# Two transformer blocks on one core: where the gates of the first block's modulation are summed, and in which order a mixer rounds its weights

## The reference, cut to what matters

```python
cond = jax.nn.silu(c)
mod = cond @ ada_w[l] + ada_b[l]
sh1, sc1, g1, sh2, sc2, g2, sh3, sc3, g3 = jnp.split(mod, N_MOD, axis=-1)
hn = _modulate(_rms_norm(h, norm_g[l, 0]), sh1, sc1)
h = h + 0.5 * g1[:, None, :] * _swiglu(hn, ffn1_w_in[l], ffn1_w_out[l])
hn = _modulate(_rms_norm(h, norm_g[l, 1]), sh2, sc2)
z = hn @ w_in[l]
```

## Time and profile before

| | |
|---|---|
| median of 3 runs | 2385.27 us (2381.89 to 2386.27) |
| the profiled execution | 2385.51 us, of which the span 2383.8 us |
| busy in the span | TensorE 2280.7, VectorE 1602.8, ScalarE 1124.5, GpSimd 121.3 us |
| mean granted clock of TensorE | 0.979 |
| read from HBM | 450.43 MB, 189 GB/s over the span |
| modulation tiles loaded | 128 of 512 KB |

### The profile page before, as it was taken

One profiled execution on the slowest core, in us unless ns is written; L12 is line 12 of the kernel. 1 busy time (PEld: TensorE's weight loads), 2 busy tenths in 40 slices (PEclk: granted clock), 3 DMA queues, 4 the chain that ended last, 5 costly groups with the idle time before them and its releaser, 6 DMA issues.

```text
span 2383.8 us, 31741 instructions
## 1 busy us (share of the span) xinstructions
PE 2280.7 (96%) x11796; PEld 1909.4 (80%) x11796; DVE 1602.8 (67%) x1813; ACT 1124.5 (47%) x1307; POOL 121.3 (5%) x174
## 2 busy tenths in 40 slices
PE   5999899999999999999999999999999999999998
PEld 3787787787788787688878889988888888998887
DVE  5886884777677687565565668686566556868655
ACT  2444454434444455444344366654445446665443
POOL 1000033000000004200000000000000000000000
PEclk9999998999999988999999999999999999999999
DMA  8896652687588473356555554446555555434553
GB/s 291 298 315 207 202 179 95 212 284 248 167 297 282 152 242 129 97 194 193 177 194 180 190 159 128 139 150 204 189 180 194 187 184 142 141 124 159 194 192 108
DMA packets 321381, 452.76 MB, mean 190 GB/s; under 512 B 32423, under 2 KB 269833, under 8 KB 320265
## 3 DMA queue, kind: packets, MB, share of 16 engines
q1 hardware_dynamic: 318232, 440.96, 56.3%
q0 software_dynamic: 2784, 9.50, 1.2%
q10 hardware_dynamic: 274, 1.06, 0.1%
HBM read 450.43 MB, written 1.05 MB: 189 GB/s over the span
## 4 chain that ended last, share of the span: by engine, by line
PE 85%; DVE 8%; ACT 3%; issue 2%; POOL 2%; POOLq 0%; DMA 0%; DVEq 0%; ACTq 0%
PE ps L558 19%; PE ps L560 19%; PE ps L559 19%; PE ps L551 4%; PE ps L552 4%; PE ps L553 4%; DVE wlo L1750 2%; PE ps L1038 2%; PE ps L662 1%; POOL side L2443 1%; PE ps L644 1%; PE ps L790 1%; PE ps L645 1%; PE ps L647 1%; PE ps L591 1%
## 5 line engine op out<-in xcount | busy, mean ns | idle before, releaser
L1750 DVE TENSOR_TENSOR wlo<-raw,whi 128x2048 fp32r<-128x2048 f32 (+1 forms) x348 | 791.6, 2278 | 396.2 <-ACT whi L1170 392.7
L1170 ACT ACTIVATE whi<-raw 128x2048 fp32r<-128x2048 f32 x346 | 660.0, 1910 | 282.3 <-PE ps L560 238.9
L558 PE MATMUL ps<-whi,xl 128*128 128x512 f32 x1472 | 593.6, 403 | 3.6 <-DVE u L1929 3.6
L560 PE MATMUL ps<-whi,xh 128*128 128x512 f32 x1472 | 575.2, 391 | 0.0
L559 PE MATMUL ps<-wlo,xh 128*128 128x512 f32 x1472 | 574.9, 391 | 0.0
L558 PEld LDWEIGHTS ps<-whi,xl 128*128 128x128 f32 x1472 | 277.2, 188 | 65.7 <-issue 4.8
L560 PEld LDWEIGHTS ps<-whi,xh 128*128 128x128 f32 x1472 | 277.1, 188 | 60.1
L559 PEld LDWEIGHTS ps<-wlo,xh 128*128 128x128 f32 x1472 | 277.5, 189 | 59.0 <-issue 4.8
L551 PE MATMUL ps<-xl,whi 128*128 128x256 f32 x864 | 254.4, 294 | 17.1 <-DVE wlo L1750 17.1
L558 PE MATMUL ps<-whi,hidl 128*128 128x512 f32 x640 | 252.2, 394 | 0.0
L560 PE MATMUL ps<-whi,hidh 128*128 128x512 f32 x640 | 249.2, 389 | 0.0
(11 more groups left out here) (375 smaller groups left out, 2553.6 us busy)
## 6 DMA issues: line engine op xcount, KB each, us to landing
raw<-in_ffn_w_in_dram SPq DMA_DIRECT2D x176, 512.0 KB
arena<-in_ada_w_dram SPq DMA_DIRECT2D x128, 512.0 KB, 5.7
raw<-in_w_in_dram SPq DMA_DIRECT2D x54, 1024.0 KB
raw<-in_ffn_w_out_dram SPq DMA_DIRECT2D x44, 1024.0 KB
raw<-in_w_ffn_gate_dram SPq DMA_DIRECT2D x88, 512.0 KB
raw<-in_w_ffn_up_dram SPq DMA_DIRECT2D x88, 512.0 KB
raw<-in_w_ffn_down_dram SPq DMA_DIRECT2D x44, 1024.0 KB
raw<-in_w_out_dram SPq DMA_DIRECT2D x16, 1024.0 KB
```

Of the source, the lines that this page charges most:

```text
L558: pe.matmul(o, al, wh, start=start, stop=False, **kw)
L560: return pe.matmul(o, ah, wh, start=False, stop=stop, **kw)
L1170: act.activation(whi[:, k % 3, :], raw[:, k % 3, :], ACT.Copy).then_inc(hi_done, 1)
L1750: tt(a[0], a[1], a[2].bitcast(F32), ALU.subtract).then_inc(lo_done, 1)
```

## The change

Sub-layers 2 and 5 take the gate path that n = 0 has (`GATED`), so the mixers 1 and 4 sum 16 tiles instead of 24 and make four pieces instead of six. `ADAM` counts the tiles of all sub-layers before m, `SUMS` the pieces. In a mixer SP puts two tile loads behind each of units 3, 4, 6, 8, 9, 10, 11 and 12, VectorE does tile sum 4 (and 5) later, rounds unit 5 inside the layer norm, with the forget logits right behind it, and its other roundings stand at other places; ScalarE rounds unit 6 ahead of the wait for the logits and unit 7 behind the square. In n = 5 the loops of VectorE and SP take the form with two groups to a turn. GpSimd zeroes and loads `accg` again in n = 2 and 5.

The counts:

```diff
+GATED = (0, 2, 5)
+ADAM = (0, 0, 24, 40, 64, 88, 104)
...
-        SUMS = (0, 4) + tuple(4 + 6 * i for i in range(1, 6))
+        SUMS = (0, 4, 10, 14, 20, 26, 30)
```

SP in the feed-forwards:

```diff
-                            if n == 0 and two is not None:
-                                sp.wait_ge(adag_used, 2 * two + (odd + 1))
+                            if n in GATED and two is not None:
+                                sp.wait_ge(adag_used, 2 * two + (KC * GATED.index(n) + odd + 1))
...
-                        if m:
+                        if m or n in GATED:
                             group(0)
                             with sp.Fori(0, KC // 2) as two:
```

SP in the mixers:

```diff
-                        for q in (2 * i - 6, 2 * i - 5):
-                            if 0 <= q < 24:
-                                sp.wait_ge(adam_used, 24 * (m - 1) + q + 1)
...
+                        first = {3: 0, 4: 2, 6: 4, 8: 6, 9: 8, 10: 10, 11: 12, 12: 14}
+                        for q in range(first[i], first[i] + 2) if i in first else ():
+                            sp.wait_ge(adam_used, ADAM[m] + q + 1)
...
+                            at = 3072 * (m % 3) + 1024 * (q % 2)
```

TensorE in the feed-forwards (`gate0` stands in the last group):

```diff
-            def gate0(q):
+            def gate0(n, q):
+                e = GATED.index(n)
                 if q == 0:
-                    pe.wait_ge(adag_used, KC + 1)
-                    pe.wait_ge(mod_read, SUMS[1] + 6)
+                    pe.wait_ge(adag_used, KC * (e + 1) + 1)
+                    if n < 5:
+                        pe.wait_ge(mod_read, SUMS[n + 2])
...
-                if n == 0:
-                    pe.wait_ge(gate0_read, 2)
+                if n in GATED:
+                    pe.wait_ge(gate0_read, 2 * GATED.index(n) + 2)
```

TensorE in the mixers:

```diff
                 project(2, 1).then_inc(unit_used, 1)
-                modulation(m, 4)
                 pe.wait_ge(s["o"], seq(L, OUTS, 4))
                 project(3, 0)
-                modulation(m, 5)
                 project(3, 1).then_inc(unit_used, 1)
```

ScalarE in the feed-forwards:

```diff
-                if n == 0:
-                    gate0(0)
-                    gate0(1)
+                if n in GATED:
+                    gate0(n, 0)
+                    gate0(n, 1)
```

ScalarE in the mixers (left out are three functions of the forget logits, then the square of dq and dk):

```diff
                 hi(L, k0 + 5)
                 copy(3)
+                hi(L, k0 + 6)
                 act.wait_ge(s["fx"], l + 1)
...
-                hi(L, k0 + 6)
                 copy(4)
-                hi(L, k0 + 7)
                 copy(5)
...
+                hi(L, k0 + 7)
                 rs(st, L.event(0), sq8h[1], stat2)
...
                 hi(L, k0 + 15)
-                summed(m, 4)
-                summed(m, 5)
```

VectorE in the feed-forwards:

```diff
-                    if n == 0 and two is not None:
-                        ada_gate(2 * two + odd)
-                if m:
+                    if n in GATED and two is not None:
+                        ada_gate(GATED.index(n), 2 * two + odd)
+                if m or n in GATED:
```

VectorE in the mixers (left out in turn: the product and the statistics; the root and the rest of the norm; the cumulated logits; the addition after the spatial mixing; the load of ypad):

```diff
                 gelu_in(1, zt["gv"], zt["cg"])
-                tiles(4, 5)
                 dve.wait_ge(s["gu_e"], 2 * l + 1)
...
+                lo(L, k0 + 5)
+                copied(L, zi["f"])
+                f, w = zt["f"][0:4, 0:S], zt["f"][0:4, S:2 * S]
+                ts(f, f, fb[0:4, l:l + 1], None, ALU.add).then_inc(s["fx"], 1)
...
-                tiles(5, 6)
-                lo(L, k0 + 5)
...
-                tiles(6, 8)
+                lo(L, k0 + 6)
+                tiles(4, 6)
+                lo(L, k0 + 7)
                 dve.wait_ge(s["fl"], l + 1)
...
-                lo(L, k0 + 6)
-                tiles(8, 10)
-                lo(L, k0 + 7)
...
-                tiles(10, 12)
                 head_norm(0, sq8h[1], diffg, ("dq", "dk"), "diffqk")
                 lo(L, k0 + 8)
-                tiles(12, 14)
-                lo(L, k0 + 9)
+                tiles(6, 8)
...
+                lo(L, k0 + 9)
                 logits(L, st, 0, S0, amask, 32 ** -0.5)
-                tiles(14, 16)
+                tiles(8, 10)
...
                 logits(L, st, 1, S1, amask, 32 ** -0.5)
-                tiles(16, 18)
+                tiles(10, 12)
...
                 gelu_in(2, zt["gu"], zt["dq"])
-                tiles(18, 20)
+                tiles(12, 13)
...
                 logits(L, st, 2, S1, amask, 1.0)
-                tiles(20, 21)
+                tiles(13, 14)
...
-                tiles(21, 22)
+                tiles(14, 15)
...
                 rest_out(L, 2, 0, 2, s0f[:, 1024:1536])
-                tiles(22, 24)
+                tiles(15, 16)
                 lo(L, k0 + 13)
```

GpSimd, after `next_gain`:

```diff
                 next_gain(n)
+                if n and n in GATED:
+                    st(pool.memset(accg, 0.0))
+                    at = 3072 * (n % 3) + 2048
+                    pool.dma_start(accg[0:1, :], ada_b[n // 3:n // 3 + 1, at:at + 1024]).then_inc(accg_init, 16)
```

More of the change, by code:

```diff
@@ L415, in tile_of @@
                             q = 3 * odd + t
-                            sp.wait_ge(adam_used, 24 * (m - 1) + 6 * two + (q + 1))
+                            sp.wait_ge(adam_used, ADAM[m] + 6 * two + (q + 1))
                             sp.sem_inc(sp_waited, 1)
@@ L754, in ffn @@
                 group(0, k, GROUPS - 3, (lambda q: modulation(m, q)) if m else None)
-                group(0, k + 3, GROUPS - 2, (lambda q: gate0(q) if q < 2 else None) if n == 0 else None, True)
+                group(0, k + 3, GROUPS - 2, (lambda q: gate0(n, q) if q < 2 else None) if n in GATED else None, True)
                 k += 7
@@ L1299, in summed, with gate0 @@
                                    scale=1.0 if m % 3 == 1 else 0.5).then_inc(mod_read, 1)
-            def gate0(q):
-                act.wait_ge(gate0_summed, q + 1)
-                act.activation(gate[:, 0, 512 * q:512 * q + 512], ps[:, MB, :], ACT.Copy,
+            def gate0(n, q):
+                act.wait_ge(gate0_summed, 2 * GATED.index(n) + q + 1)
+                act.activation(gate[:, n % 2, 512 * q:512 * q + 512], ps[:, MB, :], ACT.Copy,
                                scale=0.5).then_inc(gate0_read, 1)
@@ L1895, in ada, with ada_gate @@
             def ada(m, q, two=0):
-                at, k = q % 2, 2 * two + q // 3
-                dve.wait_ge(adam_loaded[at], (16 * (12 * (m - 1) + q // 2 + 1)) + 48 * two)
+                parts = 2 if m in (2, 5) else 3
+                at, k = q % 2, 2 * two + q // parts
+                dve.wait_ge(adam_loaded[at], (16 * (ADAM[m] // 2 + q // 2 + 1)) + 48 * two)
                 if q == 0:
                     dve.wait_ge(acc_init, 16 * m)
-                dve.wait_ge(adam_used, 24 * (m - 1) + 6 * two + (q + 2))
-                seg = acc[:, 1024 * (q % 3):1024 * (q % 3) + 1024]
+                dve.wait_ge(adam_used, ADAM[m] + 6 * two + (q + 2))
+                seg = acc[:, 1024 * (q % parts):1024 * (q % parts) + 1024]
                 scalar = condT[:, 2, bass.ds(k, 1)]
                 stt(seg, adam[:, at, :], scalar, seg, ALU.mult, ALU.add).then_inc(adam_used, 1)
-            def ada_gate(k):
-                dve.wait_ge(adag_loaded, 16 * k + 16)
-                dve.wait_ge(accg_init, 16)
-                dve.wait_ge(adag_used, k + 1)
+            def ada_gate(e, k):
+                dve.wait_ge(adag_loaded, 16 * k + (16 * KC * e + 16))
+                dve.wait_ge(accg_init, 16 * e + 16)
+                dve.wait_ge(adag_used, k + (KC * e + 1))
                 stt(accg, adag, condT[:, 2, bass.ds(k, 1)], accg, ALU.mult, ALU.add).then_inc(adag_used, 1)
```

23 lines of the change are left out of this document (10 added, 13 removed).

## The result

| | before | after |
|---|---|---|
| median | 2385.77 us of 4 runs (2381.89 to 2387.99) | 2367.35 us of 4 runs (2362.95 to 2371.32) |
| profiled execution | 2385.51 us, span 2383.8 | 2371.32 us, span 2369.6 |
| mean granted clock | 0.979 | 0.982 |

The ratio is 0.9930, its 95% interval 0.9911 to 0.9949: faster by 0.7%. The forecast was 2369.5 us, in a range of 2363 to 2378.

A forecast was written before the change was run, and what follows sets the result against it. TensorE, busy 2280.7 of 2383.8 us, was taken as the bound, its largest hole in the first mixer at unit 5. Per mixer 7.2 + 1.0 + 1.4 - 1.7 = 7.9 us, twice 15.8: 2385.3 to 2369.5 us, range 2363 to 2378.

The forecast's parts named there:

- Rounding inside the norm: Mixers 1 and 4: unit 5 rounded before TensorE needs it, so head sums start 7.2 us sooner; bounds 4.7 and 7.8.
- Does it last: After the head sums: `diffqk` done at 300.8, ahead of its scores at 301.6, a thin cover.
- The rival of a half coming back: `diffqk` or unit 10's late weights open the next hole, 3 to 4 us a mixer; 2376.5 us, chance 0.14.
- SP's loads: Unit 10's load goes out 3.3 us later, its user comes 7 us earlier; ScalarE waits 1 to 2 us before the softmax.
- An idle ScalarE for `raw`: One of the listed signs that would show the prediction wrong; no size given.
- TensorE's cost at nothing: Unit 10's late load costs TensorE nothing, with 3.5 us of slack; at most 3.3 us a mixer without that cover.
- One tile less among the taps: Last stretch of taps: three tile sums instead of four beside GpSimd's diagonals gain 1.0 us a mixer.
- The mixer's end: Last two gate sums leave the mixer, so the next sub-layer's root comes 1.4 us sooner; bounds 0.9 and 1.7.
- The feed-forwards' pieces: Gate sums moved into n = 2 and n = 5 cost TensorE 2 x 0.86 us, 1.7 us lost in each.
- The sum: Each mixer with its feed-forward gains 7.9 us; two make 15.8 us, giving 2369.5 us.
- one rival: The clock falls elsewhere: a shifted mixer gains or loses 2 to 3 us; 2375.5 or 2363.5 us, chance against 0.07.

The follow-up runs named there:

- x2: Kernel before with only the new order of roundings and logits in mixers 1 and 4, all 24 tiles and loads as before: 2417.26 us, ratio 1.0144.
- x1: Changed kernel with the old order of roundings put back in mixers 1 and 4, the gates staying moved: 2376.09 us, ratio 0.9979 to the kernel before.
- x12: Changed kernel with ScalarE's old order alone (unit 6 behind the logits' functions, unit 7 ahead of the square): 2368.74 us, ratio 0.9933 to the kernel before.
- x5: Kernel before with the new order, SP's tile loads and VectorE's tile sums moved too, 24 tiles a mixer kept: 2380.90 us, ratio 0.9981.
- x3: Changed kernel with SP's tiles 8 and 9 behind unit 10's load and later pairs moved later: 2365.26 us, ratio 0.9924 to the kernel before.
- x10: Changed kernel with taps 8 to 13 earlier, last two tile sums later, and SP's tiles 8 to 15 behind the loads of units 10 to 13: 2354.41 us.
- x11: As x5, but with SP's tiles 8 to 13 behind unit 10's load: 2383.01 us, ratio 0.9991 to the kernel before.
- x7: Changed kernel with each gate tile of n = 2 and 5 summed twice on VectorE: 2365.03 us, ratio 0.9921 to the kernel before.
- x8: Changed kernel with each mixer's last two tile sums behind GpSimd's last diagonal: 2359.52 us, ratio 0.9895 to the kernel before.
- x9: Changed kernel with taps 8 to 13 ahead of the second head sums and the last two tile sums behind GpSimd's last diagonal: 2356.51 us.

## Why the prediction was right, point by point

**Rounding inside the norm: right at the head sums, too much at the mixer's end.** Head sums predicted at 288.2, measured at 288.12; 7.2 us forecast, 7.2 and 7.5 measured. The steps too: rounding of unit 5 ends at 279.3 (279.5), the norm at 283.9 (284.2). x2 shows that the order alone does it, x1 that the tiles' places bring 1.7 to 2.4 us without it, x12 that ScalarE's part is some 1 us of it. But the forecast carried the 7.2 us to the mixer's end as the order's share of 9.6. x1 says that the order is worth 3.5 us (ledger) to 5.8 us (ratios) on top of lighter mixers, and x5 that with all 24 tiles it is worth 4.0. Each half of the change needs the other, and the sum came right because the forecast was for both together.

**Does it last: right, on the stated cover.** `diffqk` was forecast for 300.8 and ended at about 300.4, the scores started at 301.53, forecast 301.6. There is no wait. The rival of a half coming back had its place here; 24 tiles make it true (x5 lacks 6.7 of the 10.7 us, some 4.3 of them without the two gate sums and the fourth tile), 16 don't.

**SP's loads: the place right, the size wrong.** "Unit 10's load some 306.4" came at 305.69. "ScalarE then waits some 1 to 2 us" was 10.55 us. The step that failed: I set the load's later issue against today's spare time and left out that it takes 8 us more to be usable, behind two tiles of 512 KB, while ScalarE stands ready at 303.6. There was hardly any spare time: before, ScalarE used the unit at 310.86, 7.7 us after its issue, so 2.5 us later and a user 7.3 us earlier come out as 9.8 us of the 10.55. An idle ScalarE for `raw` was also named as a sign of being wrong; the sign came without its price. "TensorE's cost at nothing" held: x3 removes the wait for little, at most 1.8 us a mixer. It held because other waits lay over it; x10 shows 2.9 us once they are gone.

**One tile less among the taps: 1.0 forecast, 0.3 to 1.0 measured, by the clock.** The stretch took 27.67 before and 27.34 after (0.33), in the second mixer 27.76 and 25.65 (2.1, with clock). Of the four waits for diagonals in it, three were the same, 0.44, 1.20 and 0.61 us. The fourth is gone (0.27 us in the first mixer, 0.45 in the second), and the taps run on; before and after:

```profile
383.93 9.51 PE L1038 MATMUL ps<-arena,side 128*128 128x256 f32 x38 [0.27 <-POOL side L2443]
```

```profile
375.40 10.59 PE L1043 MATMUL ps<-arena,side 128*128 128x256 f32 x40 [0.61 <-POOL side L2441]
```

The other kernels allow a comparison at like clock. Both of the first mixer's stretches have a mean granted clock of 0.86, and there the tile is worth 0.33 us. At 0.91 the stretch takes 26.6 us with four tile sums (x5, both mixers, and x11's first) and 25.65 with three (x7, both mixers, and x12's first): 0.95 us. x8 gives 0.9 or more. An equal mean is not yet the same low stretch at the same place, but the term is right by the one pair and three times too large by the other. By the rule of the Trainium skill (SBUF — State Buffer, "Who interferes with whom") the estimate was 1.3 a tile. The like-clock figures lie below it; only x8's first mixer, with a higher clock in it, is above.

**The mixer's end: right.** From the turned probabilities of the forgetting attention on (396.03 before, 388.58 after), 8.82 - 7.45 = 1.4 us in the first mixer and 19.00 - 17.59 = 1.4 in the second, as forecast.

**The feed-forwards' pieces: right for n = 2** (1.6 to 1.8; 1.7 forecast) **and for n = 5** (1.7 at like clock; the profiled execution had another 1.4 us of low clock at the boundary, 0.54 from 986 to 993.5 us, which makes its 2.9). The tiles cost nothing, even doubled.

**The sum: right.** 15.8 forecast. In the ledger the two mixers give 8.6 + 11.7 = 20.3, minus 1.6 and 2.9 of the feed-forwards: 15.9. By the means it is 2 x 10.7 - 3.1 = 18.3, and the medians differ by 18.4. The means lie 1.1 us a mixer above the forecast 9.6, less than the 1.5 us of scatter. That the profiled sum meets the forecast to 0.1 us is luck: the first mixer gained 1.0 less than forecast, the second 2.1 more, and the clock at the boundary of n = 5 took 1.4 away.

**The clock.** In the two mixers its mean rose from 0.92 and 0.91 to 0.94 and 0.93. It fell elsewhere, as one rival said, but in a place it didn't name. In the untouched mixer n = 7 the same stretch ran at 1.00 before and at 0.91 after:

```profile
1490.00:1510.00 20.00, 16.90 (x141) 16.07 (x141) 14.54 (x16) 11.38 (x15) 0.00 (x0) 1.00 0.45 146
```

```profile
1474.00:1494.00 20.00, 16.89 (x131) 16.19 (x131) 12.91 (x15) 11.40 (x15) 0.00 (x0) 0.91 0.47 149
```

Mixer n = 7 lost 1.8 us that way. It is no effect of the change: the other kernels have 204.4 to 209.3 there in no order of their edits. That a fixed shift in time decides it was only my guess; x9 and x7 start this mixer 6.5 us apart and both have 204.4.

## What to carry to other kernels

Where a late operand opens a hole, move the rounding that feeds it ahead of work that has slack, but write down for each queue, the DMA issues' too, what stands behind what: the same order of roundings came with a gain of 10.7 us a mixer where the loads were in place and the mixer lighter, gained 4.0 with all the tiles, and lost 15 with the loads left where they were. Undo each half of a change as well as doing it alone: here the halves overlap, and neither has the price that the timeline of the whole suggests. A wait that costs nothing today can be the next limit, so try the cheap edits together as well as one by one. And compare landmark to landmark inside the traces, at like clock: the price of two small sums, which the totals hid, stood there to 0.1 us.

## What was not expected of the hardware

The stretch before the first turned x takes 37.3 to 43.6 us over 14 kernels with the same instructions there; TensorE's one wait for VectorE's first sums in it is 15.1 to 21.3 us long. That is as wide as the spread of the runs. TensorE's clock in untouched mixers moves them by 5 us without any change of the program: 204.4 us at a mean of 0.99, 209.3 at 0.96. And a diagonal on GpSimd that takes 0.37 us alone took up to 1.9 us while VectorE worked, so moving two 1.3 us instructions of VectorE out of its way, none of them removed, gained 0.9 to 1.7 us each.
